# Moving the weights' high parts and the first activation buffer by 64 bytes in a float32r transformer kernel

## What is computed

```
# first block
qkv = rms_norm(x) @ w_qkv                    # 2048 x 6144
h   = x + attention(qkv) @ w_o               # 16 heads of 128, stick-breaking weights
h   = h + square(relu(rms_norm(h) @ w1)) @ w2    # 2048 -> 8192 -> 2048
# second block, 16 meta tokens ahead of the 256
proj = rms_norm(h) @ w_in                    # 2048 x 12288: u, gb, gc, v and two gates
y_a = pool(u) @ pool_w;  y_b = (gb * conv(gc * v)) @ conv_out_w
h   = h + (g_a * y_a + g_b * y_b) @ w_o2
h   = h + (silu(gate) * up) @ w_down         # gate, up: 2048 x 5632 each
out = rms_norm(h)[16:]
```

## Time and profile before

| | |
|---|---|
| median of 3 runs | 2604.05 us (2604.03 to 2604.26) |
| profiled execution | 2604.09 us |
| its span, first to last instruction | 2602.4 us |
| PE (matmul) busy | 2592.9 us, 16309 matmuls |
| PEld (weight load) busy | 2339.4 us |
| VectorE, ScalarE, GpSimd busy | 1648.8, 1213.0, 142.7 us |
| HBM read | 481.53 MB, 186 GB/s over the span |
| TensorE clock granted | full (1.00) from the first slice to the last but the edges |

### The profile page before, as it was taken

One profiled execution on the slowest core, in us unless ns is written; L12 is line 12 of the kernel. 1 busy time (PEld: TensorE's weight loads), 2 busy tenths in 40 slices (PEclk: granted clock), 3 DMA queues, 4 the chain that ended last, 5 costly groups with the idle time before them and its releaser, 6 DMA issues.

```text
span 2602.4 us, 41094 instructions
## 1 busy us (share of the span) xinstructions
PE 2592.9 (100%) x16309; PEld 2339.4 (90%) x16309; DVE 1648.8 (63%) x1406; ACT 1213.0 (47%) x1189; POOL 142.7 (5%) x87
## 2 busy tenths in 40 slices
PE   9999999999999999999999999999999999999998
PEld 9999998888888888899899988888888888888887
DVE  6577766656656556786654776566766556655665
ACT  5455544444444444544533344444544444444444
POOL 0000100000000000000200630000000000000001
PEclk9999999999999999999999999999999999999999
DMA  7554555665565555555555555555555555555563
GB/s 263 180 175 157 164 183 180 193 191 182 193 194 183 190 193 187 185 180 190 182 187 184 178 194 182 189 194 188 184 194 193 184 188 194 193 183 189 194 205 118
DMA packets 243953, 485.24 MB, mean 186 GB/s; under 512 B 7728, under 2 KB 8944, under 8 KB 243696
## 3 DMA queue, kind: packets, MB, share of 16 engines
q1 hardware_dynamic: 243520, 483.12, 57.0%
q10 hardware_dynamic: 320, 0.53, 0.1%
HBM read 481.53 MB, written 2.10 MB: 186 GB/s over the span
## 4 chain that ended last, share of the span: by engine, by line
PE 99%; DVE 1%; issue 0%; ACT 0%; POOL 0%; DVEq 0%; ACTq 0%; POOLq 0%
PE ps L1325 46%; PE ps L1331 24%; PE ps L1345 14%; PE ps L1353 7%; PE ps L1313 4%; PE ps L1319 2%; PE ps L1455 0%; PE ps L1401 0%; PE ps L1367 0%; PE ps L1389 0%; PE ps L1460 0%; PE ps L1438 0%; PE ps L1238 0%; PE ps L1392 0%; PE ps L1248 0%
## 5 line engine op out<-in xcount | busy, mean ns | idle before, releaser
L762 DVE TENSOR_TENSOR wlo<-raw,whi 128x1024 fp32r<-128x1024 f32 x900 | 1135.8, 1271 | 901.1 <-ACT whi L555 899.4
L555 ACT ACTIVATE whi<-raw 128x1024 fp32r<-128x1024 f32 x900 | 951.9, 1060 | 1300.1 <-PE ps L1331 969.9
L1325 PE MATMUL ps<-b_buf,whi 128*128 128x512 f32 x2688 | 670.2, 391 | 0.0
L1325 PE MATMUL ps<-a_buf,whi 128*128 128x512 f32 x2560 | 645.6, 394 | 0.0
L1325 PEld LDWEIGHTS ps<-b_buf,whi 128*128 128x128 f32 x2688 | 480.6, 188 | 82.9
L1325 PEld LDWEIGHTS ps<-a_buf,whi 128*128 128x128 f32 x2560 | 459.6, 188 | 85.0
L1331 PEld LDWEIGHTS ps<-b_buf,wlo 128*128 128x128 f32 x2688 | 359.3, 188 | 27.8
L1331 PEld LDWEIGHTS ps<-a_buf,wlo 128*128 128x128 f32 x2560 | 346.9, 188 | 27.0
L1331 PE MATMUL ps<-b_buf,wlo 128*128 128x256 f32 x2688 | 365.6, 278 | 0.0
L1331 PE MATMUL ps<-a_buf,wlo 128*128 128x256 f32 x2560 | 354.3, 281 | 0.0
L1345 PE MATMUL ps<-a_buf,whi 128*128 128x258 f32 (+4 forms) x2560 | 330.9, 282 | 0.0
(11 more groups left out here) (190 smaller groups left out, 1052.8 us busy)
## 6 DMA issues: line engine op xcount, KB each, us to landing
raw<-in_mlp_w_dram SPq DMA_DIRECT2D x128, 1024.0 KB, 5.1
raw<-in_w_in_dram SPq DMA_DIRECT2D x96, 1024.0 KB, 5.0
raw<-in_w_gate_up_dram SPq DMA_DIRECT2D x88, 1024.0 KB, 5.0
raw<-in_sb_w_qkv_dram SPq DMA_DIRECT2D x44, 1024.0 KB, 5.1
raw<-in_w_down_dram SPq DMA_DIRECT2D x44, 1024.0 KB, 5.1
raw<-in_sb_w_o_dram SPq DMA_DIRECT2D x16, 1024.0 KB, 5.1
raw<-in_conv_out_w_dram SPq DMA_DIRECT2D x16, 1024.0 KB, 5.1
raw<-in_w_o_dram SPq DMA_DIRECT2D x16, 1024.0 KB, 5.1
```

Of the source, the lines that this page charges most:

```text
L555: act.activation(whi[:, unit_of(n, u)], raw[:, n % RAW, u * UK:(u + 1) * UK, :], ACT.Copy).then_inc(w_hi, 1)
L762: dve.tensor_tensor(wlo[:, s], raw[:, n % RAW, u * UK:(u + 1) * UK, :], cast(whi[:, s]), ALU.subtract).then_inc(w_lo, 1)
L1325: pe.matmul(ps[:, 4 * half + j, :].rearrange("p (a n) -> p a n", a=2), whi[:, s, kt, j * P:(j + 1) * P], buf[:, :, x, tok], start=first an ...
```

## The change

`wlo` changes places with `whi`, and the gap of 64 bytes that lay ahead of `b_buf` now lies ahead of `whi`. `whi` and `a_buf` so lie 64 bytes further on in phase, `wlo` keeps its phase, and `b_buf` and all that follows keep their addresses. No instruction is added, removed or moved on any engine.

```diff
         raw, _ = place("raw", [P, RAW, KT, PW])
+        wlo, _ = place("wlo", [P, SPLIT, UK, PW], F32R)
+        top[0] += 64
         whi, _ = place("whi", [P, SPLIT, UK, PW], F32R)
-        wlo, _ = place("wlo", [P, SPLIT, UK, PW], F32R)
         a_buf, _ = place("a_buf", [P, 2, NT, TW], F32R)
-        top[0] += 64
         b_buf, b_off = place("b_buf", [P, 2, NT, T], F32R)
```

## The result

The changed kernel takes 2610.93 us (median of 10 runs, 2610.49 to 2611.18), the kernel before 2604.28 (10 runs beside them, 2604.03 to 2604.56): a ratio of 1.0025, with a 95% interval of 1.0017 to 1.0034. It is slower by 6.65 us, where +10.0 was forecast.

What follows compares the result with a forecast made beforehand. The prediction took PE's pace from one matmul's start to the next as the bound, PE being busy 2592.9 of 2602.4 us. Its terms, 8.1 + 1.9 + 0 + 0 = +10.0 us, gave 2614 us, range 2601 to 2628.

Steps and rivals of the forecast that it cites:

- The prediction's own signs: Right if `b_buf` stage +0.8 us, L1325 there 394 ns; wrong if L1331 there leaves 278 or `a_buf` stage moves over 0.3 us.
- Term (1): High weights by `b_buf`, 512 columns: distance 64 to 0 bytes, 3 ns on each of 2688 matmuls, +8.1 us.
- The row of tile 7: Four in-phase 512-column matmuls on `a_buf` with mean 394 ns, against 391 on `b_buf`; gave the 3 ns price.
- Term (3): Low weights by `b_buf`: distance 64 before and after, taken as 0, with -5.4 to +5.4 us depending on the hand-over.
- The case behind the bound of +5.4: Low matmuls by `b_buf`: all 336 units at the slow pace, half of them losing 4 ns a matmul, +5.4 us.
- Term (2): High weights by `b_buf`, 256 columns, placed in the `pw` stage: 640 matmuls at 3 ns more, +1.9 us.
- Term (4): `a_buf` by high and low weights: distance unchanged or mean over the tiles unchanged, 0.
- My bound of 2.6 us: Allowance on `a_buf`: 1 ns either way on the 2560 matmuls of L1331, +-2.6 us.
- Term (5): ScalarE and VectorE: `raw` and `whi` go from in phase to 64 bytes apart; any effect covered by their idle time.
- Nothing happening: Rival: `a_buf`'s slower pace could come from its 1088-byte rows, so 2604 us, or up to +5 us; chance 0.27.
- The fast lock of the low matmuls: Rival: low matmuls by `b_buf` all take the fast pace, -5.4 us, about 2600 us in all; chance 0.08.
- The worse steady run: Rival: in-phase high matmuls by `b_buf` cost 6 ns and all low ones go slow, about 2626 us; chance 0.20.

Runs made afterwards that it cites:

- e3: Kernel before with the 64-byte gap moved behind `b_buf`, so `whi`, `wlo`, `a_buf` and `b_buf` share one phase: 2618.32 us, ratio 1.0055.
- e10: Kernel before, same addresses, each paired chunk issuing sixteen high then sixteen low matmuls instead of eight and eight twice: 2604.56 us, ratio 1.0004.
- e1: Kernel before with `whi` alone moved 64 bytes on in phase: 2614.27 us, ratio 1.0040.
- e2: Kernel before with `a_buf` alone moved 64 bytes on in phase: 2608.78 us, ratio 1.0019.
- e11: Kernel before with `a_buf` and `b_buf` at phase 256, `whi` and `wlo` still at 128: 2622.91 us, ratio 1.0074.
- e7: Kernel before with `raw` alone moved to phase 192, behind the gap and ahead of `b_buf`: 2603.93 us, ratio 1.0002.
- e5: Kernel before with `raw`, `whi`, `wlo`, `a_buf` and `b_buf` all 1088 bytes further on, distances among them unchanged: 2603.82 us, ratio 1.0002.
- e6: Changed kernel with 256 bytes more between `b_buf` and both `whi` and `a_buf`, distances modulo 256 unchanged: 2610.83 us.
- e4: Kernel before with `wlo` alone moved 64 bytes on, into phase with `b_buf`: 2609.92 us, ratio 1.0023.
- e12: Changed kernel with sixteen high and then sixteen low matmuls per paired chunk: 2608.63 us, ratio 1.0019 against the kernel before.

## Why the prediction was right, and where it was not

The direction, the place (PE's own pace, no wait) and the range held: 2610.93 us in 2601 to 2628, where the forecast was 2614. The mechanism held in its first half, that the distance between the moving operand and the weights sets the pace, and not in its second, that each group can be priced by its own distance. The prediction's own signs say the same: the `b_buf` stage is 0.86 us longer (0.8 forecast), but its L1325 reads 392 and not 394, its L1331 left 278 for 280, and the `a_buf` stage moved by 0.37 us, over the 0.3 that it had set.

**Term (1), high weights by `b_buf`, was mis-sized: +8.1 us, measured +2.8.** The row of tile 7 holds four matmuls that come from another distance. I had named this, and e3 shows what it hid: a settled run in phase goes at 389 ns, 2 ns below the 391 of 64 apart. The +1 ns on the mean is the way to that pace, which each unit begins anew after its low matmuls.

**Term (3), low weights by `b_buf`, was mis-sized: 0, measured +6.2 us in the paired stages and -1.4 in `w_o` and `pw`.** The case behind the bound of +5.4, all units at the slow pace, is what happened, and 6.2 is even above it. It was my own "it matters how the high matmuls leave the two readers standing" that decided. e10 shows that the hand-over picks the pace, since the same addresses and a longer group move the fast pace from every second unit to every second chunk. With `whi` and `wlo` at different distances the fast low pace is gone in paired stages on `b_buf` (with the change in all 336 groups, in e1 in all but 8). That (1) and (3) together give +9.0 where 8.1 was forecast is luck: the sum was right and its parts were not.

**Term (2), high weights in 256 columns: +1.9 us, measured +1.4** from start to start (75.6 to 77.0 us). The count of 640 belongs to `w_o` and `pw`, not to `pw` alone as I wrote. The reading from `values` was right, since that run was a settled one. But the low matmuls beside them paid it back (38.1 to 36.7 us), which I had put at 0.

**Term (4), `a_buf`: 0, measured -3.7 us in paired stages, +1.2 and +0.7 in the others.** The step that failed is "the tiles go through all four distances before and after, so the mean stays". e2 and e11 show it directly: the same distances in other pairs cost 0.32 us a stage, in the same pairs nothing. My bound of 2.6 us was too narrow for the paired stages. This term is also what brought the total down from near the forecast +10.0 to +6.65.

**Term (5) held:** ScalarE and VectorE are busy as before, and e7 shows that their side of the addresses does not reach TensorE.

**The rivals.** Nothing happening is out by the result and by e5, e6 and e1: equal distances give equal stages, to 0.02 us, wherever the buffers lie. The Trainium skill ("SBUF — State Buffer", Who interferes with whom) calls PE's two read ports independent. What the prediction drew from it, that no distance between their addresses moves TensorE's pace, does not hold for this kernel: e3 against the kernel before is 14.4 us of span from 64 bytes of distance. That PE waits on no other engine is not refuted here: e7 and the settled pace in e3 agree with it. The fast lock of the low matmuls does exist, in `w_o` and `pw`, where it made exactly up for the high ones. The worse steady run came in its one half, the low matmuls all at the slow pace, and not in its other: what is steady in phase with 512 columns is fast.

What stays open is which of the two reads is held up by the other, and why the pattern has a period of 256 bytes. That the partner is the weight load follows by exclusion: of all that touches `whi` and `wlo`, ScalarE's and VectorE's instructions leave the settled pace as it is (the comparison in e3). The last high matmul of a unit in e4 points to it directly: its own two operands lie as in the kernel before, only the load beside it is of `wlo`, and it is the slow one. No run varied the load alone. Distances that are no multiple of 64 were not tried.

## What to carry to other kernels

In this kernel, where TensorE hardly waits, the distance between its moving operand and its weights in a partition is worth up to 0.7%: with the same instructions in the same order the kernels tried take 2604 to 2623 us. A term for it can't be read from a few matmuls in passing: take a long run at one distance, and look at the groups on both sides of the one you change, since most of the loss fell on matmuls whose own distance had not moved. The length of a stage, from start to start, repeats to 0.02 us here, and tells apart in one profile what times with an interval of 0.1% can't.

## What the hardware showed

Equal matmuls with equal distances have more than one pace, and keep it: 256 columns at 64 bytes apart go at 113.3 or at 117.8 ns from start to start, for a whole group, according to how the group ahead ended (e10). In phase they go at 120.0 (e3). For 512 columns the order is reversed: 226.7 ns in phase once settled, against a round of 226, 229 and 232 at 64 apart. After the low matmuls it takes five high ones to reach the settled pace in e3, where all distances are equal, and ten in e12, where they are not.
